# Hybrid RG-LRU, pooling, Fourier and MoE trunk: pooling tiles projected first, late modulation rows on TensorE, a twice folded Fourier transform

## The reference

```python
mod_lat = silu(c) @ mod_w + mod_b          # 6 rows of 1024: shift, scale, gate; shift, scale, gate
mod_ctx = silu(c_ctx) @ mod_w + mod_b      # rows 0 and 1 are used
hc = modulate(rms_norm(ctx, g), mod_ctx[0], mod_ctx[1])
sf, sb = last states of recurrent_branch(hc @ w_in[:, :512], zero states)
z = modulate(rms_norm(x, g), mod_lat[0], mod_lat[1]) @ w_in      # 1536 columns
y_a = (forward + backward RG-LRU of conv(z[:, :512]), from sf, sb) * gelu(z[:, 512:1024])
y_p = ((box means over rows and columns, windows 2, 4, 8, 16, of z[:, 1024:1280]) - itself) @ pool_w * pool_scale
y_f = real(fft2(z[:, 1280:1536] as 4 heads of 64, over tokens and head channels, ortho)) @ fourier_w
x = x + mod_lat[2] * (concat(y_a, y_p, y_f) @ w_out)
x = x + mod_lat[5] * moe(modulate(rms_norm(x, g2), mod_lat[3], mod_lat[4]))
                                            # top group of 4, top 2 of its 4 experts, SwiGLU, width 512
out = rms_norm(x, final_g)
```

## Time and profile before

| | us |
|---|---|
| median of 3 runs | 962.16 (959.39 to 962.84) |
| the profiled execution | 960.46 |
| its span, first to last instruction | 958.7 |
| TensorE busy | 832.5 (87%) |
| VectorE busy | 650.9 (68%) |
| ScalarE busy | 421.2 (44%) |
| GpSimd busy | 200.3 (21%) |
| mean granted clock of TensorE | 0.938 of full speed |

### The profile page before, as it was taken

The page is one execution under the profiler, slowest core; times in us unless marked ns, Lnnn a source line. Parts: engine busy times, 40 slices in busy tenths (PEclk is TensorE's granted clock), DMA queues, the critical chain, the costliest instruction groups (busy, mean ns, idle before and its releaser), DMA issues.

```text
span 958.7 us, 11551 instructions
## 1 busy us (share of the span) xinstructions
PE 832.5 (87%) x3625; PEld 587.7 (61%) x3626; DVE 650.9 (68%) x706; ACT 421.2 (44%) x522; POOL 200.3 (21%) x192
## 2 busy tenths in 40 slices
PE   2599999965979898999928999999999999999980
PEld 1364444422534555888716888788878888778860
DVE  2233778998689154445587879658877579946856
ACT  2333533433444342213335467435746358624553
POOL 1000561970000000000003113312242214432120
PEclk9599999987989999999958999999999999999996
DMA  9913603303520451353366699796996699975766
GB/s 361 323 31 131 219 22 110 109 0 109 172 78 15 175 197 67 112 204 125 110 236 237 242 346 378 231 323 200 354 369 182 232 299 396 360 234 160 264 231 264
DMA packets 85767, 196.73 MB, mean 205 GB/s; under 512 B 10739, under 2 KB 23153, under 8 KB 85740
## 3 DMA queue, kind: packets, MB, share of 16 engines
q1 hardware_dynamic: 76992, 165.39, 47.6%
q0 software_dynamic: 7056, 25.15, 10.5%
q10 hardware_dynamic: 1692, 5.85, 1.5%
HBM read 172.27 MB, written 24.64 MB: 205 GB/s over the span
## 4 chain that ended last, share of the span: by engine, by line
PE 56%; DVE 17%; DMA 13%; issue 6%; ACT 4%; POOL 1%; DVEq 1%; ACTq 1%; POOLq 1%; SPq 0%
PE bank L790 11%; PE bank L1022 5%; PE bank L1024 5%; PE bank L1023 5%; DMA mixed_rows<-ysc,idg 4%; DMA xt<-in_x 3%; PE bank L916 3%; PE bank L917 3%; PE bank L918 3%; PE bank L1043 3%; PE bank L1045 2%; PE bank L1044 2%; DMA xg<-normed_rows,idg 2%; PE bank L833 2%; DVE U L1502 2%
## 5 line engine op out<-in xcount | busy, mean ns | idle before, releaser
L1633 DVE TENSOR_TENSOR gu<-raw_gu,gu 128x2048 fp32r<-128x2048 f32 x64 | 145.4, 2287 | 34.4 <-ACT gu L1286 34.3
L790 PE MATMUL bank<-hT,wring 128*128 128x512 f32 x384 | 166.8, 593 | 1.7 <-ACT hT L1118 1.0
L1022 PE MATMUL bank<-gu,xp 128*128 128x512 f32 x368 | 147.2, 400 | 3.8 <-issue 2.4
L1286 ACT ACTIVATE gu<-raw_gu 128x2048 fp32r<-128x2048 f32 x64 | 122.6, 1918 | 54.5 <-PE bank L1024 47.9
L1024 PE MATMUL bank<-gu,xp 128*128 128x512 f32 x368 | 144.9, 394 | 0.0
L1023 PE MATMUL bank<-gu,xp 128*128 128x512 f32 x368 | 144.6, 393 | 0.0
L790 PEld LDWEIGHTS bank<-hT,wring 128*128 128x128 f32 x384 | 72.7, 190 | 90.8 <-issue 88.5
L1793 DVE TENSOR_TENSOR dn<-raw_dn,dn 128x1024 fp32r<-128x1024 f32 x64 | 76.0, 1223 | 10.9 <-ACT dn L1322 9.0
L1022 PEld LDWEIGHTS bank<-gu,xp 128*128 128x128 f32 x368 | 70.1, 191 | 18.2 <-issue 2.6
L1024 PEld LDWEIGHTS bank<-gu,xp 128*128 128x128 f32 x368 | 69.9, 190 | 15.0
L1023 PEld LDWEIGHTS bank<-gu,xp 128*128 128x128 f32 x368 | 70.2, 191 | 13.9
(11 more groups left out here) (301 smaller groups left out, 1330.8 us busy)
## 6 DMA issues: line engine op xcount, KB each, us to landing
raw_gu<-in_expert_w_gate SPq DMA_DIRECT2D x64, 512.0 KB, 6.8
raw_gu<-in_expert_w_up SPq DMA_DIRECT2D x64, 512.0 KB, 7.9
raw_dn<-in_expert_w_down SPq DMA_DIRECT2D x64, 512.0 KB, 10.1
mring<-in_mod_w SPq DMA_DIRECT2D x18, 1024.0 KB, 5.5
mfirst<-in_mod_w SPq DMA_DIRECT2D x6, 1024.0 KB, 23.5
wring<-in_w_in SPq DMA_DIRECT2D x12, 512.0 KB, 6.5
xt<-in_x ACTq DMA_DIRECT2D x2, 2048.0 KB, 27.5
dring<-in_dft SPq DMA_DIRECT2D x8, 512.0 KB, 4.1
```

Source lines behind the costliest of these rows:

```text
L790: mm = pe.matmul(o_, wring[:, n % 3, k, :], src, start=k == 0, stop=k == KD - 1)
L1022: pe.matmul(bank[g][:], x_hi, w_hi, start=k == 0, stop=False)
L1286: A_(gu[j][0][:], raw_gu[j][:], ACT.Copy).then_inc(s_hgu, 1)
L1633: tt(gu[j][1][:], raw_gu[j][:], gu[j][0][:].bitcast(F32), ALU.subtract).then_inc(s_logu[j], 1)
```

## The change

It leaves everything from the second output tile on as it is. Ahead of that:

- **Input order.** x goes first, context last: ACT issues only the first half of x; SyncE the second half and the context, between w_in tiles. The first projections are the half tiles of both pooling tiles, with the transposes of the second half of x and of the context between them. `hT` is stored by halves of tokens.
- **Late modulation rows.** `mod_pair(j)` multiplies two pieces by silu(c) as one-column weights into partitions 0, 32, 64 and 96 of bank 7, and adds the bias by a matmul of a unit column with the parameter rows. ACT copies the sums (`mod_row`); SyncE stores a row in DRAM (`store_row`) and loads it back spread over the partitions (`spread_row`). `mod_sums`, `mod_product` and `mod_end` are gone.
- **Rounds.** Order on TensorE: x, pair, g, pair, gates. ACT takes the root of round i-1 after the context part of x, and gelu's tanh after the gates; DVE goes through one round after the other.
- **Fourier.** DVE folds the 1024 tokens twice (`fold`: sums and differences of token n and 1024-n, even and odd tokens apart), so the table has 512 rows of 512 columns and one row of alternating signs; it is loaded whole. `four_sums` makes the four quarters of the output tokens.
- **Pieces.** y0 to y5 are split first, then w, then y6 and y7; w_out is loaded by halves as the halves of `hT` come free. The first output tile's two halves run up to k=5 and are finished later.

```diff
+    turn = lambda a, b: 2 * np.pi * (np.outer(a, b) % SEQ) / SEQ
+    q = HALF // 2
+    even, odd = np.arange(0, HALF, 2), np.arange(1, HALF, 2)
+    dft = np.zeros((HALF + 1, HALF))
+    dft[0:q] = np.concatenate([np.cos(turn(even, np.arange(q + 1))), np.sin(turn(even, np.arange(1, q)))], axis=1)
+    dft[q:HALF] = np.concatenate([np.cos(turn(odd, np.arange(q))), np.sin(turn(odd, np.arange(1, q + 1)))], axis=1)
+    dft[HALF, 0:q + 1] = 1.0 - 2.0 * (np.arange(q + 1) % 2)
...
-        COLT = [("x", 0), ("g", 0), ("p", 0), ("x", 1), ("g", 1), ("p", 1), ("x", 2), ("g", 2), ("x", 3), ("g", 3),
+        SPLIT = [("y", k) for k in range(6)] + [("w", k) for k in range(KD)] + [("y", 6), ("y", 7)]
+        COLT = [("p", 0), ("p", 1), ("x", 0), ("g", 0), ("x", 1), ("g", 1), ("x", 2), ("g", 2), ("x", 3), ("g", 3),
...
+            load_win(0)
+            load_win(1)
+            sp.dma_start(xt[:, 4:8], xv[:, 4:8]).then_inc(s_x[1], 16)
+            load_win(2)
+            sp.dma_start(ctxt[:], ctx[0].rearrange("(t p) d -> p t d", p=P)).then_inc(s_x[2], 16)
...
+            for n in range(2):
+                load_mod(2 * MCH + n)
             for n in range(3, len(COLT)):
                 load_win(n)
-                for _ in range(2):
-                    if mod_next < NMC - 2:
...
+                if n >= 5:
+                    load_mod(2 * MCH + 2 * (n - 4))
+                    load_mod(2 * MCH + 2 * (n - 4) + 1)
+                if n in (7, 9, 11):
+                    store_row((n - 7) // 2)
+                if n in (8, 10):
+                    spread_row((n - 8) // 2)
+            spread_row(2)
+            store_row(3)
+            sp.wait_ge(s_modp, 4 * MCH)
+            sp.dma_start(gff[:], everywhere(norm_ffn_g[0:1])).then_inc(s_scin, 16)
+            spread_row(3)
...
+            sp.dma_start(dalt[:], dft[HALF:HALF + 1]).then_inc(s_dalt, 16)
+            sp.dma_start(dtab[:], dft[0:HALF].rearrange("(k p) n -> p k n", p=P)).then_inc(s_dft, 16)
+            sp.dma_start(xr[0][:], xv[:, 0]).then_inc(s_xr[0], 16)
+            for h in range(2):
+                sp.wait_ge(s_z, UNIT[(COLT[-1], h)] + 1)
+                sp.dma_start(wout_sb[:, 4 * h:4 * h + 4],
+                             w_out[0].rearrange("(k p) n -> p k n", p=P)[:, 4 * h:4 * h + 4]).then_inc(s_wout[h], 16)
+            sp.wait_ge(s_dftu, 2)
...
+            for n in range(6):
                 first_mod(n)
-            pe.wait_ge(s_xs, 2)
-            for k in range(KD):
...
+            mod_columns(0)
+            pe.wait_ge(s_xs, 4)
+            for n in range(KD - 2):
+                turn_in(n)
             first_mod(6)
             first_mod(7)
-            pe.wait_ge(s_mcol, 2)
-            for m in range(2):
...
+            mod_columns(1)
...
+            z_unit(0, 0)
+            z_unit(1, 0, range(0, 4))
+            pe.wait_ge(s_xs, 8)
+            for n in range(KD, KD + 4):
+                turn_in(n)
+            z_unit(1, 0, range(4, KD))
+            for n in range(KD + 4, 2 * KD):
+                turn_in(n)
+            z_unit(0, 1)
             pe.wait_ge(s_xs, 10)
-            for n in range(KD, KD + 4):
-                turn_x(n)
...
+            for n in range(2 * KD, 2 * KD + 4):
+                turn_in(n)
+            z_unit(1, 1, range(0, 4))
+            for n in range(2 * KD + 4, 3 * KD):
+                turn_in(n)
+            z_unit(1, 1, range(4, KD))
...
+            def mod_pair(j):
+                i = j // 2
+                if j % 2 == 0 and i:
+                    pe.wait_ge(s_mrow, i)
+                for n in (2 * MCH + 2 * j, 2 * MCH + 2 * j + 1):
+                    pe.wait_ge(s_mod[n % 2], 16 * mod_fill(n))
+                    for h in range(2):
+                        k = 2 * (n % MCH) + h
+                        for c4 in range(4):
+                            mm = pe.matmul(bank[7][32 * c4:32 * c4 + 1, 0:256], silu_c[:, 0, k:k + 1],
+                                           mwide[n % 2][:, h, 256 * c4:256 * c4 + 256], start=k == 0, stop=False)
+                    mm.then_inc(s_modp, 1)
+                if j % 2:
+                    for c4 in range(4):
+                        for h in range(2):
+                            r = PV["modb"][0] + KD * MORD[i + 2] + 2 * c4 + h
+                            mm = pe.matmul(bank[7][32 * c4:32 * c4 + 1, h * P:(h + 1) * P], ident[0:NPV, r:r + 1],
+                                           prow[0:NPV, :], start=False, stop=h == 1)
+                    mm.then_inc(s_mprod, 1)
...
+            def feature_product(m):
+                pe.wait_ge(s_fold, m + 1)
+                for j in range(2):
+                    u = NU + 2 * m + j
+                    pe.wait_ge(s_zu, u - 3)
+                    for i in range(2):
+                        for g in range(2):
+                            a = (2 * i + g) * P
+                            mm = pe.matmul(bank[u % 4][:, a:a + P], zfold[m][:, g, j, i * P:(i + 1) * P],
+                                           csw[m][:, g * P:(g + 1) * P], start=True, stop=True)
+                    mm.then_inc(s_z, 1)
+            def token_transform(m):
+                pe.wait_ge(s_zu, NU + 2 * m + 2)
+                pe.wait_ge(s_dft, 16)
+                if m == 0:
+                    pe.wait_ge(s_py, 4)
+                for i in range(4):
+                    b, w = FB[m][i // 2], 257 - i // 2
+                    pe.matmul(b[:, 0:w], Vf[:, m, i, 0], dtab[:, i, 0:w], start=i % 2 == 0, stop=False)
+                    pe.matmul(b[:, w:], Vf[:, m, i, 1], dtab[:, i, w:], start=False, stop=i == 3)
+                pe.wait_ge(s_vmc, m + 1)
+                pe.wait_ge(s_dalt, 16)
+                pe.matmul(FB[m][0][:, 0:257], vmid[:, m], dalt[:, 0:257], start=False, stop=True).then_inc(s_dftu, 1)
...
-            for n, ct in enumerate(COLT):
-                if n:
...
+            mod_pair(0)
+            for i in range(NI):
+                if i:
+                    z_tile(2 * i + 2)
+                    mod_pair(2 * i)
+                z_tile(2 * i + 3)
+                mod_pair(2 * i + 1)
+                gates(i)
+            z_tile(10)
+            pool_products()
+            middle_row(0)
+            z_tile(11)
+            feature_product(0)
+            pe.wait_ge(s_scr, 1)
+            pe.wait_ge(s_shin, 16)
+            for j in range(2 * KD):
+                src = (scr, shr)[j // KD]
+                mm = pe.transpose(bank[4][:, 2 * j:2 * j + 2], src[0:2, j % KD * P:(j % KD + 1) * P], ident[0:2, 0:2])
+            mm.then_inc(s_ct, 1)
+            token_transform(0)
+            middle_row(1)
+            feature_product(1)
+            pe.wait_ge(s_shb, 1)
+            for j in range(KD):
+                mm = pe.matmul(bank[4][:, 64:64 + NG + NE], shb[:, j, :], rw[:, j, :], start=j == 0, stop=j == KD - 1)
+            mm.then_inc(s_cp, 1)
+            token_transform(1)
...
+            out_half(0, 0, range(0, 6))
+            out_half(0, 1, range(0, 6))
+            out_half(0, 0, range(6, KD))
+            out_half(0, 1, range(6, KD))
+            for t in range(1, NT):
...
+            for i in range(NI):
+                take_x(i, ("c",))
+                if i:
+                    rec_root(i - 1)
+                take_x(i, (0, 1))
+                take_g(i)
+                mod_row(i)
+                rec_gates(i)
+                gelu_tanh(i)
...
+            take_f(0, 0)
+            take_f(0, 1)
             for q in range(4):
                 m, h = q // 2, q % 2
                 act.wait_ge(s_pm, q + 1)
                 A_(yT[:, 4 * h:4 * h + 4, 4 + m, :], bank[6 + q % 2][:].rearrange("p (t n) -> p t n", n=P), ACT.Copy,
                    scale=V("psc", m)).then_inc(s_py, 1)
-            def split_hi(i):
-                what, k = SPLIT[i]
...
+            take_middle(0)
             act.wait_ge(s_y, NI)
-            act.wait_ge(s_z, NU + NT)
-            for i in range(EARLY):
+            for i in range(4):
                 split_hi(i)
-            act.wait_ge(s_dftu, NT)
-            for m in range(2):
-                A_(xm[m][:, 0:HALF], bank[m][:], ACT.Copy).then_inc(s_fc, 1)
-            for i in range(EARLY, 2 * KD):
+            take_f(1, 0)
+            split_hi(4)
+            split_hi(5)
+            take_f(1, 1)
+            take_v(0)
+            take_v(1)
+            split_hi(6)
+            split_hi(7)
+            take_middle(1)
+            take_v(2)
+            take_v(3)
+            split_hi(8)
+            split_hi(9)
+            take_even(0)
+            for i in range(10, 13):
+                split_hi(i)
+            take_even(1)
+            for i in range(13, 16):
...
-            def mod_sums(m):
-                for q in range(MCH):
-                    n = MORD.index(m) * MCH + q
-                    dve.wait_ge(s_mod[n % 2], 16 * mod_fill(n))
-                    for h in range(2):
-                        k = 2 * q + h
-                        ck = silu_c[:, 0, k:k + 1]
```

(58 more changed lines are left out.)

459 lines of the change are left out of this document (169 added, 290 removed).

## The result

| | before | after |
|---|---|---|
| median, us | 962.5 (959.39 to 963.08, 4 runs) | 905.08 (904.36 to 906.68, 4 runs) |
| ratio | | 0.9402, 95% interval 0.9367 to 0.9436 |
| the profiled execution, us | 960.46 | 906.68 |
| its span, us | 958.7 | 904.9 |
| TensorE, VectorE, ScalarE, GpSimd busy, us | 832.5, 650.9, 421.2, 200.3 | 808.5, 597.5, 420.3, 193.6 |

The kernel is 57.4 us faster by the medians.

The account below looks back on a forecast made before the run. TensorE was taken as the bound, with gaps waiting for VectorE and a nearly serial tail. 16.6 us up to the last projection plus 38.9 in the tail, 55.5, took 960.46 to 905; 2 for hand-overs made 907, range 895 to 926.

Parts of the forecast that it names:

- Loading: Start of the kernel: scale and shift ready at 42.5 against 48.3, first x tile at 78; gives 8 us.
- Modulation rows: Late modulation rows on TensorE in each round: 4.3 us a round, 17.2 in all, bounds 14 to 29.
- Pooling beside round 0: GpSimd pooling stretches VectorE until 155, so TensorE waits 5.5 us before gates 1, range 3 to 16.
- Gates at 11.0: Gate part of each round on TensorE: 11.0 us of a 46.7 us round.
- Tail: Last projection's end to output tile 0's end: 29.5 us against 68.4, 38.9 less, with TensorE ahead of VectorE.
- Why VectorE was late before: TensorE's gaps at 205 to 230, one of 9.2 us: VectorE late from modulation sums and stretching by pooling.
- The sum: Whole stretch up to VectorE taking output tile 0's second half, at 387.05 before: 16.6 + 38.9 = 55.5 us earlier.
- The 2 us for hand-overs: Added to 905 for some fifteen new hand-overs of 0.1 to 0.2 us, giving 907.
- the column groups': Rival: late modulation matmuls don't overlap, 0.43 instead of 0.11 each, +41 less 5.5: 943 us; chance 0.04.
- The clock rival: Rival: narrow work and waits for ACT keep TensorE's clock low in the rounds, 76 us lost: 983; chance 0.03.
- Thin covers: Rival: pooling stretches scans and conv 1 (+10), w_out late or folds and sums double (+8): 922; chance 0.16.
- the expert stretch moved with the event: Rival claimed the contrary: expert stretch starts 55 us earlier but waits for something not shifted, about 960; chance 0.02.

Follow-up runs that it names:

- the run with one group: Changed kernel with all 128 late modulation matmuls writing to one partition of one column group (rows wrong): 945.64 us in one run.
- the table early: Changed kernel with a one-column tanh on ScalarE between the copies of x and g each round, loading tanh's table there: 907.15 us, ratio 0.9435.
- the run with four times the transform: Changed kernel with the folded token transform's products summed four times over, values unchanged: 922.36 us, ratio 0.9593.
- 8-column sums: Kernel before the change, 28 of VectorE's 32 late modulation sum instructions cut to 8 columns: VectorE takes output tile 0's second half at 385.24 us, against 387.05.

## Why the prediction came out right, step by step

- **Loading** was to give 8 us. x tiles 0 to 3 landed at 23.5 (23.3 forecast), scale and shift were there at 40.5 (42.5), the first x tile started at 75.1 (78): 2.9 better. The clock was mostly up, 0.86 in the window that had 0.59 in the earlier trace rows, where I had taken a middle; and scale and shift came even before my bound for the high clock (41.6), since copy, columns and additions behind the last pieces took 1.9 us (38.6 to 40.5), less than I had left for them. Undone, the queue order costs 6.0 at the first projection.

```profile
24.00:48.00 24.00, 18.23 (x120) 11.41 (x121) 7.48 (x18) 12.68 (x24) 0.00 (x0) 0.86 1.00 324
```

- **Modulation rows** at 4.3 us a round: 4.1 measured, and the run with one group shows why: fourfold.
- **Pooling beside round 0.** The wait before gates 1 was forecast at 5.5, within 3 to 16; it was 1.54, below the range, and 3.2 in the three profiles without a dip in gates 0, which pushes TensorE's arrival back. Loading and GpSimd share the rest: pooling started at 72.9 and took 71.5 us, not 78.5, since its own instructions are short while VectorE idles (2.13 us against 3.46 of the earlier trace rows). Gates 1 started at 161.1, not 166.
- **Gates at 11.0** was the term mis-sized. They took 13.5, 13.0, 12.0 and 13.7 us, 8.2 more in sum. Without a dip they take 12.0, and with the table early and no dip 10.9 (110.13 to 121.06), so 1.1 a round is the table load, which before the change came with gelu's tanh and now is awaited at the head of the gates ("costs ACT nothing that is awaited" was wrong); the rest is the clock, 4.1 of its 5.1 in the gates and 1.0 in the projection behind them. From the start of gates 1 to the last projection's end this is 141.7 against my 136.1: 5.6 lost, which the 4.9 up to gates 1 repaid. The last projection ended at 302.8 against 302.1: two errors of 5 us that cancel, not precision.
- **Tail**: 29.5 forecast, 28.8 measured. Folds took 1.5 for 2 and sums 3.0 for 3.5. That VectorE alone sets it, with TensorE ahead, was wrong: TensorE is busy without a gap from 302.8 to 326.5, VectorE waits for ACT up to 303.7 (2.55) and again 4.70, and the run with four times the transform passed on 18.7 of 20.7 us. By these rows two engines bind it in turn, handed over by ACT's copies.
- **Why VectorE was late before**: I named the sums and pooling alike. In the rounds the runs show pooling (-13.8 us), the order on ACT (-3.3) and the width of the sums (-1.6), each taken alone and in one profile each, with the clock's dips of 1.7 in them. They share one gap, so they don't add, and whether all three together close it was shown only by the changed kernel, where nothing of it is left; the late sums together with pooling were not taken out.
- **The sum**, 55.5, met 55.45 at the event. The 2 us for hand-overs have no row of their own; 1.65 lost in the expert stretch stand in their place, by luck.

Of the rivals, the column groups' failed in its condition, since they do overlap; its price was right, 35.5 said and 36.2 measured with one group. The clock rival's mechanism exists, narrowly: 5.1 us in three dips, not 76. Thin covers: only the wait before gates 1; ACT waited 0.43 us for w_out. And the expert stretch moved with the event but for 1.65 us, so it waited for nothing that stayed.

## What to carry to other kernels

An engine that waits a fixed 2 us for another in each round can be filled with independent work of that size; look for it in the same queue before shortening the waited-for engine. Dips of the clock that stand behind such waits may be part of their price. A gain made ahead of a point that another engine sets (here convolution 1) is not passed on: look for the next wait that will grow before counting it. And when a sum comes out right, compare it term by term, since errors of one part can pay for those of another.

## What was not expected of the hardware

- A wait of 1.97 us is followed by a loss of clock in some executions and not in others of the same program: 17.16 instead of 15.48 us for the stretch. Ten runs of it spread over 10 us, of which the dips in the rounds are a part. One profile can't show the price of such a wait.
- Four column groups with one-column fp32 weights run fully side by side: 0.108 us a matmul of 256 columns against 0.43.
- The port is paid for on both sides. GpSimd's addition of 1264 columns takes 2.13 us with VectorE idle and 3.2 beside it (12.71 for four), VectorE's of 1280 takes 1.49 alone and up to 3.66 beside pooling. The Trainium skill's "SBUF — State Buffer", section "SBUF: two separate sides", calls the shared pair an exclusive lock; this trace agrees in that both lose. The 8-column sums of 4.27 us, where those without pooling beside them take 0.23, say the same.
- A scan instruction takes 2.83 us alone, and took 4.86 where it stood partly beside pooling (the profile with the table early, GpSimd done at 145.4), a price that no row of before showed:

```profile
143.16 4.86 DVE L1605 TENSOR_TENSOR_SCAN RH<-AA,IH 128x1280 f32<-128x1280 f32 x1
```
